# Two transformer blocks on one core: norm chains shared by ScalarE and VectorE, first loads in another order, second block unrolled, gates in groups of eight

## The reference

```
h = rms_norm(x, norm_mix_pre);  proj = h @ w_in          # 1024 -> 6560
o = diff_attention, moba_attention, latent attention     # three branches of 512
mixed = (sum_g sigmoid(gate_g) * (o_g @ w_branch_g)) @ w_out
x = x + rms_norm(mixed, norm_mix_post)
h = rms_norm(x, norm_mlp_pre)
x = x + rms_norm(square(relu(h @ w_up)) @ w_down, norm_mlp_post)
```

## Time and profile before

| | |
|---|---|
| median of 3 runs | 3406.91 us |
| the profiled execution, its own time | 3410.91 us |
| its span, first to last instruction | 3409.1 us |
| mean granted TensorE clock | 0.935 of full |
| PE, DVE, ACT, POOL busy | 88%, 60%, 35%, 9% |
| DMA | 524 MB, 154 GB/s mean |

### The profile page before, as it was taken

The page is one execution under the profiler, slowest core; times in us unless marked ns, Lnnn a source line. Parts: engine busy times, 40 slices in busy tenths (PEclk is TensorE's granted clock), DMA queues, the critical chain, the costliest instruction groups (busy, mean ns, idle before and its releaser), DMA issues.

```text
span 3409.1 us, 50117 instructions
## 1 busy us (share of the span) xinstructions
PE 2994.2 (88%) x17202; PEld 2547.7 (75%) x17202; DVE 2040.5 (60%) x3762; ACT 1200.4 (35%) x1740; POOL 309.5 (9%) x432
## 2 busy tenths in 40 slices
PE   7864799999999888558999999996989796999798
PEld 3653688899999765447999999985874785976596
DVE  4659966777777632997666666654542654543464
ACT  0201744444444311156444444433430332431232
POOL 0007810000000000663000000000000000000000
PEclk9887999999999987889999999997999897999899
DMA  7531045666666531102555555544332353323353
GB/s 269 187 131 69 0 144 197 226 228 229 225 230 226 195 114 55 69 0 88 189 187 186 187 185 186 188 156 177 119 132 109 138 185 126 142 110 131 112 185 136
DMA packets 130152, 524.08 MB, mean 154 GB/s; under 512 B 19261, under 2 KB 27325, under 8 KB 107257
## 3 DMA queue, kind: packets, MB, share of 16 engines
q1 hardware_dynamic: 115688, 502.62, 42.8%
q10 hardware_dynamic: 14354, 20.01, 1.9%
HBM read 519.41 MB, written 3.16 MB: 153 GB/s over the span
## 4 chain that ended last, share of the span: by engine, by line
issue 55%; PE 30%; DVE 12%; DVEq 1%; DMA 1%; ACT 1%; POOL 0%; ACTq 0%; POOLq 0%; SPq 0%
PE prob_ps L1054 11%; PE acc L1065 10%; DVE slab L2135 3%; PE acc L742 3%; PE acc L763 2%; DVE arena L2079 1%; DVE arena L2070 1%; DVE arena L2073 1%; DVE slab L2138 1%; PE turn_ps L868 1%; DVE arena L2094 1%; DVE arena L2076 1%; DVE arena L2067 1%; PE prob_ps L1039 1%; PE turn_ps L813 0%
## 5 line engine op out<-in xcount | busy, mean ns | idle before, releaser
L1054 PEld LDWEIGHTS prob_ps<-hTr,utr 128*128 128x128 f32 x6144 | 776.9, 193 | 36.1 <-issue 17.5
L1054 PE MATMUL prob_ps<-hTr,utr 128*128 128x256 f32 x6144 | 788.5, 285 | 10.6 <-DVE utr L2147 6.1
L1065 PE MATMUL acc<-vr,wtr 128*128 128x512 f32 x3072 | 748.4, 392 | 5.3 <-DVE vr L2165 5.3
L1065 PEld LDWEIGHTS acc<-vr,wtr 128*128 128x128 f32 x3072 | 562.7, 189 | 112.8 <-issue 6.2
L2165 DVE TENSOR_TENSOR vr<-slab,vr 128x1024 fp32r<-128x1024 f32 x256 | 313.6, 1225 | 440.4 <-ACT vr L1539 440.4
L1539 ACT CAST vr<-slab 128x1024 fp32r<-128x1024 f32 x256 | 268.4, 1048 | 608.2 <-PE acc L1065 608.2
L2147 DVE TENSOR_TENSOR utr<-slab,utr 128x1024 fp32r<-128x1024 f32 x256 | 311.7, 1218 | 11.7 <-ACT utr L1525 11.7
L1753 POOL TENSOR_TENSOR small<-small 128x2 f32<-128x2 f32 (+3 forms) x18 | 21.7, 1204 | 2908.7 <-DVE small L1793 2009.9
L813 PE MATMUL turn_ps<-ident,arena 128*128 128x128 f32 (+1 forms) x336 | 68.0, 362 | 231.1 <-DVE arena L1311 93.3
L1525 ACT CAST utr<-slab 128x1024 fp32r<-128x1024 f32 x256 | 267.4, 1045 | 4.6 <-issue 4.6
L813 PEld LDWEIGHTS turn_ps<-ident,arena 128*128 128x128 f32 (+1 forms) x336 | 52.2, 184 | 253.3 <-issue 100.3
(11 more groups left out here) (233 smaller groups left out, 4556.9 us busy)
## 6 DMA issues: line engine op xcount, KB each, us to landing
slab<-in_pack_b SPq DMA_DIRECT2D x132, 1024.0 KB, 4.9
slab<-in_peer_u SPq DMA_DIRECT2D x256, 512.0 KB, 4.6
slab<-in_peer_v SPq DMA_DIRECT2D x256, 512.0 KB, 3.5
arena<-in_pack_a SPq DMA_DIRECT2D x84, 512.0 KB, 4.6
slab<-in_pack_a SPq DMA_DIRECT2D x40, 1024.0 KB, 7.0
slab<-in_pack_b SPq DMA_DIRECT2D x4, 832.0 KB, 5.3
arena<-in_pack_a SPq DMA_DIRECT2D x2, 1024.0 KB, 17.3
arena<-in_norm_g ACTq DMA_DIRECT2D x4, 512.0 KB, 7.2
```

The lines of the kernel that those rows point to most:

```text
L1054: ins = pe.matmul(prob_ps[:, m % 2, 0:S], utr[:, m % 2, uh, k * P:k * P + P], hTr[:, hh, k, :], start=(k == 0 and n == 0), stop=(k == KD - ...
L1065: ins = pe.matmul(y_ps[:, t, n, :], wtr[:, m % 2, wh, t * P:t * P + P], vr[:, vh, n * 512:n * 512 + 512], start=first and k == 0, stop=las ...
```

## The change

It has seven parts. (1) c comes as 128 rows of 8, first in SP's queue; positions and small constants are packed on the host, four constants remain; the bias matmul closes each group; the angles move behind the first transposes. (2) In each norm ACT squares and sums (`x_squares`, `row_squares`, `acc_squares`) while DVE multiplies by the gain; `variance` adds the parts; the scale and shift become one instruction; x is updated tile by tile or half by half; output banks are squared and scaled where they lie in PSUM. (3) `ada_first(7)` and `(8)` move behind the second norm of a0, their sums on PE beside the scores. (4) `TOKG` 8, `STEP` 4: 32 groups in 8 rounds of 4; the rows are made 4 by POOL, 2 by ACT, 2 by DVE, and a group fills two banks of `acc`. (5) The second block is written out twice; SP may load b1's first slabs when b0's last ones are used; the bias is loaded in 16 parts during a1's expert loop (ACT's loop is split in two for it), the small parameters on SP behind slabs dk and dv. (6) The low parts of h go ahead of those of the weights on DVE, and ACT scales one tile of h. (7) PE takes the two products with the high weight first and waits for the low weight only then.

```diff
-TOKG = 4
-STEP = 8
-POOLQ = 2
+TOKG = 8
+STEP = 4
+POOLQ = 4
+ACTQ = 2
-N_CONSTS = 6
+N_CONSTS = 4
...
         def slabs_a(sp, l):
+            if l == 0:
+                sp.dma_start(cT, io["c_turned"]).then_inc(c_in, 16)
...
             if i >= 2:
                 lay, prev, blk = l, names[i - 2], block
-            elif block == "a":
-                return
+            elif block == "b" and l > 0:
+                lay, prev, blk = l - 1, names[i - 2], block
...
                     for i in (2, 3, 0):
-                        pe.matmul(dst, ones, bias0[:, 512 * i:512 * i + 512], start=True, stop=False)
...
                         for k in range(KD):
-                            ins = pe.matmul(dst, cbc[:, k, :], w(k), start=False, stop=(k == KD - 1))
+                            pe.matmul(dst, cbc[:, k, :], w(k), start=(k == 0), stop=False)
+                        if i == 2:
+                            pe.wait_ge(tiles_clear, 1)
+                            pe.wait_ge(start_bias, 16)
+                        pe.matmul(dst, ones, bias0[:, 512 * i:512 * i + 512], start=False, stop=True)\
...
+            def x_squares(key, tiles, scratch):
+                act.wait_ge(x_part, X_PARTS_AT[key])
+                for src, total in tiles:
+                    act.activation(scratch[:, 0:src.shape[-1]], src, ACT.Square, scale=D ** -0.5, accum_out=total)
+                    act.drain()
+                act.drain().then_inc(squared, 1)
+            def row_squares(layer, prefix, scratch):
+                for t in range(T):
+                    x_squares((layer, f"{prefix}{t}"), [(x[:, t], sq[:, 0, t:t + 1])], scratch)
...
+                    for q in range(ACTQ):
+                        act.activation(key_gap[:, q], iota[:], ACT.Square, bias=keys[:, at + q:at + q + 1], scale=-1.0)
                     act.drain()
+                    for q in range(ACTQ):
+                        ins = act.activation(rows[:, j % 2, 1, POOLQ + q, :], key_gap[:, q], ACT.Relu, bias=1.0, scale=-1.0)
+                    ins.then_inc(act_rows.sem, 1)
...
-                    with act.Fori(0, NKEYS // 4 - 1) as it:
+                    with act.Fori(0, 15) as it:
...
+                    load(pre_gain.sem, wpre, wide(io["norm_mix_pre_2"][0], D))
+                    with act.Fori(0, 16) as it:
+                        for j in range(4):
+                            block_of(it, 4, 63 + j)
+                            if j == 1:
+                                load(bias_in, bias.rearrange("p h t s -> p (h t s)")[:, bass.ds(it * 256, 256)],
+                                     bias_dram[:, bass.ds(it * 256, 256)])
...
+                if l > 0:
+                    proj_split(0)
+                row_squares(DEPTH + l, "t", junk)
+                if l == 0:
+                    proj_split(0)
+                half_scaled(1)
...
+                def acc_squares(use, n):
+                    act.wait_ge(*accs.full_at("b", l, use))
+                    k = BANKS.index(use) + 1
+                    act.activation(junk[:, 0:512], nat("b", use)[:, 0], ACT.Square, scale=D ** -0.5, accum_out=sq[:, n, 0:1])
+                    act.drain().then_inc(bank_squared.sem, 1)
+                    act.wait_ge(*bank_scaled.at("b", l, k))
+                    act.activation(junk[:, 0:512], nat("b", use)[:, 1], ACT.Square, scale=D ** -0.5, accum_out=sq[:, n, 1:2])
+                    act.drain().then_inc(squared, 1)
...
                 slab_high(0)
+                row_squares(DEPTH + l, "m", junk)
+                half_scaled(5)
...
+            def modulated(block, l, k, shift):
+                        ins = dve.scalar_tensor_tensor(hn[:, t, cols], hn[:, t, cols], rstd[:, t:t + 1], shift[:, cols],
+                                                       ALU.mult, ALU.add)
+            def variance(block, l, key, halves):
+                dve.wait_ge(squared, SQUARES_AT[key])
+            def rows_normed(layer, prefix, k, gain):
+                dve.tensor_tensor(bn[:, 0], x[:, 0], gain, ALU.mult)
+                variance("b", layer - DEPTH, (layer, f"{prefix}1"), False)
+                dve.tensor_tensor(bn[:, 1], x[:, 1], gain, ALU.mult)
+                dve.drain()
+                dve.wait_ge(*rstd_ready.at("b", layer - DEPTH, k))
+                dve.tensor_scalar(bn[:, 1], bn[:, 1], rstd[:, 1:2], None, ALU.mult).then_inc(h_ready.sem, 1)
...
-                    if l == 0 and n == 1:
-                        ada_first(7)
-                        ada_first(8)
+                    if l == 0 and n == 0:
                         dve.wait_ge(ada_kept, 6)
...
+                    x_done()
+                    dve.tensor_tensor(hn[:, :, cols], x[:, :, cols], spread(gain2[:, cols], 1, T), ALU.mult)
+                variance("a", l, (l, "x1"), True)
...
                 for g in (1, 3):
                     keep_turned(dve, "a", l, f"h2_{g}", hT[:, 2 * g:2 * g + 2, :])
+                if l == 0:
+                    ada_first(7)
+                    ada_first(8)
...
-            with dve.Fori(0, DEPTH) as l:
+            for l in range(DEPTH):
...
+                def add_normed(stem, k, gain, more=True):
+                    for n in range(GC):
+                        dve.tensor_tensor(bn[:, 1, cols], nat[:, 1], gain[:, cols], ALU.mult).then_inc(bank_scaled.sem, 1)
+                        dve.wait_ge(*bank_squared.at("b", l, BANKS.index(use) + 1))
+                        dve.tensor_tensor(bn[:, 0, cols], nat[:, 0], gain[:, cols], ALU.mult)
+                    variance("b", l, (DEPTH + l, f"{stem}1"), True)
...
+                        dve.scalar_tensor_tensor(x[:, t], bn[:, t], rstd[:, t:t + 1], x[:, t], ALU.mult, ALU.add)
```

302 lines of the change are left out of this document (160 added, 142 removed).

## The result

The changed kernel takes 3315.39 us, median of 4 runs (3311.54 to 3318.47), where the kernel before took 3408.98 beside it (3406.6 to 3414.21). The ratio is 0.9722, 95% interval 0.971 to 0.9734: 93.6 us less. The forecast was 3322 with a range of 3300 to 3345. The profiled executions are 3410.91 and 3314.98, spans of 3409.1 and 3313.2; they differ by 95.9, against 85.1 in the sum.

The account below looks back on a forecast made before the run. PE, 88% busy, was taken as the bound, so only stretches where PE stands still could gain; the ten steps sum to 85.1 us, off the 3406.9 median: 3322 us, range 3300 to 3345.

Parts of the forecast that it names:

- steps 1 to 8: The start, the joints between stages and the tail: shorter chains and waits there save 87.6 us in all.
- step 1: Start: c first in SP's queue, so PE's first real matmuls begin at 8.3 instead of 16.91; 8.7 us saved.
- step 2: Second norm of a0: without DVE's wait for a piece, 12.0 us replace 30.8; 18.8 saved, minus 0.5 behind it.
- step 5: Joint a1 to b0, 33.0 us: no wait for the first gain, matmuls start at 16.4; 16.6 us saved.
- step 6: Joint b0 to b1: 14.6 us replace 33.8, with the 4.65 us loop-end stall gone; 19.0 saved.
- Step 7: Output projection to MLP in b, twice: 16.0 us replace 24.2; 8.2 saved each, 16.4 in all.
- Step 9: Gate stages: groups of eight keep the same pace; plus 1 us a layer, bounds minus 7 and plus 8.
- Rival (b): Gates gain after all through fewer hand-overs: minus 7 us a layer instead of plus 1, 3306 us; chance 0.18.
- rival (d): Gates: the ring of two groups locks as DVE, POOL and PE alternate; plus 173 us, 3495 us; chance 0.03.
- Step 10: Expert loop of a1: sixteen 128 KB loads issued by ACT cost nothing, or 8 us if ACT's cover fails.
- Rival (a): Joints give less, through engine crossings, late slabs or table loads: 2.5 us more at nine places, 3344 us; chance 0.20.
- Rival (c): In a0 SP stands at slab 8's pieces before loading wq2, and PE waits: 12 us returned, 3334 us; chance 0.05.

Follow-up runs that it names:

- The two last edits: Against the changed kernel: one DVE instruction for b's second normed tile (3321.4 us); only half of up0 split before the squares (3312.57 us); together 11.7 us less.
- the run with the stall put back: Changed kernel with ada_first(7) and (8), PE's two sums and ACT's copies back between out0 and out1 of a0: 3331.05 us, ratio 0.977.

## Why the prediction was right

**The joints (steps 1 to 8).** Each was priced as a chain of rows of before plus a Square of 1.3, and measured within 1.0 us: 9.7 for 8.7, 19.4 for 18.8, 2.7 and 2.3 for 2.0, 16.7 for 16.6, 18.4 for 19.0, 14.8 in two joints for 16.4, 4.4 for 4.1. A Square of 1024 columns takes 1.06 and its sum 0.19, of 512 0.63 and 0.19: the assumed 1.3 and 0.85 were right. The experiments bear out the causes of steps 1, 2 and 5 one by one, and that of the loop's 4.65 in step 6.

Two of the matches are closer than their terms. In step 5 the turns were to start at 10.6, the slab's landing at 8.7 plus its cast of 1.9; the scale of 1.0 behind the cast was left out of that sum. The slab came 1.3 earlier, at 7.4, and the scale took 1.14, so the turns started 10.5 behind a1's last matmul: two errors that cancel. In step 1 PE began at 9.27 for 8.3, and ada2's sixteen matmuls took 8.93 for 10.7, which makes up for it. Step 6's own chain of 14.6 gives 19.2 rather than 19.0 saved, and step 2's terms add up to 11.8 rather than 12.0.

**Step 7 was the worst sized**, 0.8 short in each of two joints. The forecast had ACT's 3.7 us of casts cover DVE's work; they end 1.4 us behind the first tile of x and hold its square up. It also priced variance and root at 1.1; they take 2.0, as the root's row is 1.60 with DVE's multiply beside it. The two last edits gave back 1.95 in each joint by removing just these.

**Step 2's cover.** The slabs stayed under wq0, as forecast, with 7.33 us to spare on DVE. The forecast priced what comes behind at 0.5; the whole stretch to the experts, gates and all, took 2.4 more than before in one execution of the changed kernel and 0.5 less in the other. In the run with the stall put back 2.2 us of the difference are wq0's clock. Net of these the move gave 13.8 there; the whole kernel gave 15.7.

**Step 9, the gates:** the forecast's plus 1.0 a layer is in the changed kernel's first execution and not in all others: over ten executions the mean is that of groups of four within 0.4 us. What the forecast put at nothing is the expert loop behind it, 0 to 4 us in a1. Rival (b), minus 7 a layer, and rival (d), the locked ring, did not show: the rows took 95.2 us for 95.6 and 96.2.

**Step 10:** the loads in a1's loop cost nothing, and bring nothing. Rival (a) showed in step 7, 1.6 us in all, and in step 6, 0.6. Rival (c) did not show: SP stood, PE did not.

**Table loads.** They are seven after, eight before, at 1.28 each, and none stands between a square and the next step of a chain; L1675 above lies under PE's matmuls. A Square behind Gelu or Exp brought no load of its own here, so the warning taken from the Trainium skill, ScalarE: Activation LUTs (Table sets: the hidden batching unit), had nothing to bite on; no run shows what two sets in turn would cost. The forecast set the row's 1.28 against the page's 2.7 as if both were the load: by the same page of the Trainium skill (What ACT_TABLE_LOAD costs) the larger figure takes in a drain behind a load of 1283 ns, and the rows agree with that load.

**What the sum missed** is 10.8 us of the profiled times: 0.8 in the joints, 10.0 between them. The mean granted clock is 0.935 before and 0.949 after: twice the difference to 1, times the span, makes 443 and 338 us at 1.2 GHz. Of the 105 us less at half speed much was idle time in the joints that went; the rest fell on stretches that shrank with no edit in them. That the clock made them shorter is shown for the experts of a1 (the windows above: the same 4608 matmuls at 0.99 and at 1.00) and for 4.1 of the 5.5 us of a1's mixer in the version with both edits; for the others it is argued. Why the clock differs from one execution to the next stays open. The forecast counted only waits, and took every stretch between joints at its old length. On a second execution of the changed kernel 3.9 us of the extra gain, in a1's experts, were gone again; so how near the time came to 3322 is in part luck, and the joints are what was forecast.

## What to carry to other kernels

Cut the span at the same matmuls in both traces and judge an edit by its joint, which repeated to 0.02 us in one kernel and to 0.3 over all of them, not by the time of one run, which here moves by 9 us with the clock; the joints of 33 us fell to half when squares, gains and root run on three engines and the load it needs first is first in its queue. Then look in the new trace for the engine that came late (ACT's casts) and for two engines that slow each other (POOL beside a DVE instruction with two inputs): the two gave 4.7 us in the joints. Where a move puts work under another stage, look in that stage for the engine that it waits for: here DVE stood 7.33 us behind the moved work, so it was covered, and what the stage lost was clock on PE.

## What the runs showed of the hardware

- POOL's root of 128x2 elements takes 0.69 to 0.73 us with DVE standing and 1.60 to 1.63 with a DVE multiply of two tensors beside it; the same four places changed with the DVE instruction alone.
- DVE stood 4.65 us at the head of a loop's second turn, and 0.13 with the loop written out.
- How much of a stretch runs at 1.2 GHz differs between executions and between kernels that are equal in that stretch: 119.9 to 126.3 us for a1's mixer, 27.7 or 30.1 for the 64 matmuls of an output projection in b, 5.98 to 8.72 for the same first 48 matmuls of a1's experts. The edit that won 5.6 us at one joint (the unrolled block) lost 4.7 in two such gemms in the same execution.
- A drain behind a 0.31 us ACT row, with one buffer in place of two ahead of it, made a gate stage 3 us longer: ACT's row became the last of a group in 68 of PE's waits, and in none without them.
- ACT brought 1024 single elements of c 14.2 us after their issue; as 128 rows of 8 on SP's queue they landed in 1.6. Form and queue were changed together.
